# Loads brought forward over layer ends, own credits for up and down, and the last square summed on TensorE, in a two-stack transformer kernel

## What is computed

```python
for l in range(DEPTH):                      # first stack, DEPTH = 2
    h = mixer_sublayer(h, mix_pre_g[l], mix_post_g[l], w_in[l], ..., w_out[l])
    h = ffn_sublayer(h, ffn_pre_g[l], ffn_post_g[l], ffn_w_up[l], ffn_conv_w[l], ffn_w_down[l])
# mixer_sublayer: u = rms_norm(h, pre_g); z = u @ w_in; attention, convolutions; y @ w_out
#                 return h + rms_norm(y, post_g)
# ffn_sublayer:   z = conv(rms_norm(h, pre_g) @ w_up); y = (silu(g) * up) @ w_down
#                 return h + rms_norm(y, post_g)
...
# second stack, per layer: h = h + mixers(_rmsnorm(h, norm_attn_2)) @ w_out_2
#                          h = h + relu(_rmsnorm(h, norm_mlp_2) @ w_up_2) ** 2 @ w_down_2
# output: _rmsnorm(h, final_norm_2)
```

## Time and profile before

| what | value |
|---|---|
| median of 3 runs | 3361.15 us (3355.04 to 3365.78) |
| the profiled execution | 3370.27 us, of it the span 3368.3 us |
| TensorE matmul busy | 88% of the span, 18018 matmuls |
| VectorE, ScalarE, GpSimd busy | 44%, 32%, 8% |
| mean granted clock of TensorE | 0.899 of full speed |
| DMA | 235.90 MB, mean 70 GB/s |
| a 1 MB load of the ring | 4.8 us from issue to landing |

### The profile page before, as it was taken

How to read it: one execution, slowest core, us unless ns; L and a number is a source line. 1 busy time by engine, 2 the same in 40 slices (tenths; PEclk the granted TensorE clock), 3 DMA queues, 4 the chain that set the end, 5 groups by cost and what they waited for, 6 DMA issues and landing times. The chain is left out here.

```text
span 3368.3 us, 47839 instructions
## 1 busy us (share of the span) xinstructions
PE 2973.7 (88%) x18018; PEld 2573.7 (76%) x18018; DVE 1475.2 (44%) x2316; ACT 1066.9 (32%) x1482; POOL 259.1 (8%) x230
## 2 busy tenths in 40 slices
PE   6897899896988899988898886999979878789998
PEld 5886899896986799987695555877768755567776
DVE  3642577613553377722323543423332245433332
ACT  3234433322234333322322223323232222333232
POOL 1000200003000200002000012000010001200001
PEclk8988999998988899999896778999989767789999
DMA  3200322221210322221421001222222200022222
GB/s 111 93 19 26 119 87 87 75 92 52 88 50 1 118 87 89 79 86 38 156 88 38 1 1 50 87 93 95 87 84 97 75 1 1 26 75 87 96 90 76
DMA packets 43930, 235.90 MB, mean 70 GB/s; under 512 B 4286, under 2 KB 14142, under 8 KB 20752
## 3 DMA queue, kind: packets, MB, share of 16 engines
q1 hardware_dynamic: 33968, 220.92, 18.9%
q10 hardware_dynamic: 9824, 13.16, 1.2%
HBM read 231.91 MB, written 11.59 MB: 72 GB/s over the span
## 5 line engine op out<-in xcount | busy, mean ns | idle before, releaser
L163 PE MATMUL psum<-u_up_a_hi,w_a_hi 128*128 128x264 f32 x1408 | 377.8, 288 | 19.9 <-DVE u_up_a_lo L1688 16.9
L164 PE MATMUL psum<-u_up_a_lo,w_a_hi 128*128 128x264 f32 x1408 | 374.0, 286 | 0.0
L154 DVE TENSOR_TENSOR w_mlp_b_lo<-ring,w_mlp_b_hi 128x1024 fp32r<-128x1024 f32 x128 | 156.8, 1225 | 384.5 <-ACT w_mlp_b_hi L147 384.5
L154 DVE TENSOR_TENSOR w_a_lo<-ring,w_a_hi 128x1024 fp32r<-128x1024 f32 x150 | 186.0, 1241 | 254.3 <-ACT w_a_hi L147 251.9
L163 PEld LDWEIGHTS psum<-u_up_a_hi,w_a_hi 128*128 128x128 f32 x1408 | 265.8, 189 | 28.9 <-DVE u_up_a_lo L1688 21.9
L166 PE MATMUL psum<-u_up_a_hi,w_a_lo 128*128 128x264 f32 x1408 | 286.5, 285 | 0.0
L164 PEld LDWEIGHTS psum<-u_up_a_lo,w_a_hi 128*128 128x128 f32 x1408 | 265.2, 188 | 0.2
L147 ACT ACTIVATE w_a_hi<-ring 128x1024 fp32r<-128x1024 f32 x150 | 158.3, 1056 | 320.7 <-PE psum L166 320.5
L147 ACT ACTIVATE w_mlp_b_hi<-ring 128x1024 fp32r<-128x1024 f32 x128 | 136.1, 1063 | 348.5 <-PE psum L166 347.7
L163 PE MATMUL psum<-u_up_b_hi,w_mlp_b_hi 128*128 128x512 f32 x512 | 203.4, 397 | 24.7 <-DVEq L500 24.7
L166 PEld LDWEIGHTS psum<-u_up_a_hi,w_a_lo 128*128 128x128 f32 x1408 | 220.1, 189 | 0.0
(11 more groups left out here) (405 smaller groups left out, 6845.5 us busy)
## 6 DMA issues: line engine op xcount, KB each, us to landing
ring<-in_wup SPq DMA_DIRECT2D x44, 1024.0 KB, 4.8
ring<-in_wup_b SPq DMA_DIRECT2D x32, 1024.0 KB, 4.8
ring<-in_wdown_b SPq DMA_DIRECT2D x32, 1024.0 KB, 4.9
ring<-in_win SPq DMA_DIRECT2D x24, 1024.0 KB, 4.8
ring<-in_wdown SPq DMA_DIRECT2D x32, 704.0 KB, 4.1
ring<-in_win_b SPq DMA_DIRECT2D x16, 1024.0 KB, 4.9
near_copies<-near_rows ACTq DMA_DIRECT2D x2, 4608.0 KB
ring<-in_wout SPq DMA_DIRECT2D x8, 1024.0 KB, 4.8
```

The costliest lines, as they stand in the source:

```text
L154: nc.vector.tensor_tensor(W["lo"][:, buf, 0:n], W["tiles"][:, slot, at:at + n], W["hi"][:, buf, 0:n].bitcast(F32), ALU.subtract).then_inc( ...
L163: nc.tensor.matmul(out[c], a_hi, b_hi, start=start, stop=False)
L164: nc.tensor.matmul(out[c], a_hi, b_lo, start=False, stop=False)
```

## The change

- The ring's two fill semaphores now belong to both stacks and count through. The first stack's down stage and the second stack's last down product load the next layer's first two slots (`win_next`, `win_b_next`); the start stage loads those of the first layer. The constants that used the ring as a staging place get places of their own. The last layer loads two slots that nobody reads.
- The gains of the scaling come from a small table of their own (`pre_gain`), loaded one stage or more ahead. The large column table is waited for after the second low part.
- In the first stage of each layer, the first lot's high part comes before the rounding of h, and its low part after the second scaled tile. The load of ScalarE's table for logarithm and exponential comes after the second high part. The turning of the far rows comes after lot 0.
- Up and down of the second stack have semaphores of their own (`up_free`, `down_free`), down uses banks 4 and 5, and all first credits are given at the beginning of the stage.
- GpSimd sums the first seven squares only; TensorE multiplies the total, then the last square, into the same bank. In `linear_stage` ScalarE squares before it copies.
- In `layer_end_a` VectorE adds to h, one tile behind its scaling.

```diff
-def first_slots(eng, ring, source):
-    for s in range(2):
-        w = source(s)
-        eng.dma_start(ring["tiles"][:, s, 0:w.shape[-1]], w).then_inc(ring["full"][s], 16)
 def slot_full(ring, layer, base, j):
-    return layer * (ring["per_layer"] // 2 * 16) + (j * 16 + (base // 2 + 1) * 16)
+    return layer * (ring["per_layer"] // 2 * 16) + (ring["full_base"] + j * 16 + (base // 2 + 1) * 16)
...
-            pe.wait_ge(added.sem, added.at(layer, 9 * use + 9))
+            pe.wait_ge(added.sem, added.at(layer, KD * use + KD))
             for c, (c0, cn) in enumerate(chunks(T)):
-                mm = nc.tensor.matmul(ps[:, 6 + c, 0:cn], S["mean_mat"][:, :], total[:, c0:c0 + cn], start=True, stop=True)
+                nc.tensor.matmul(ps[:, 6 + c, 0:cn], S["mean_mat"][:, :], total[:, c0:c0 + cn], start=True, stop=False)
+            pe.wait_ge(made.sem, made.at(layer, KD * use + KD))
+            for c, (c0, cn) in enumerate(chunks(T)):
+                mm = nc.tensor.matmul(ps[:, 6 + c, 0:cn], S["mean_mat"][:, :], sq[:, c0:c0 + cn], start=False, stop=True)
             mm.then_inc(summed.sem, 1)
...
-                    nc.scalar.activation(split(out[:, it * tiles + t, 0:T], T), banks(ps, wide * b, T), ACT.Copy)
-                    act.wait_ge(added.sem, added.at(layer, it * tiles + (9 * use + t + 1)))
+                    act.wait_ge(added.sem, added.at(layer, it * tiles + (KD * use + t + 1)))
                     nc.scalar.activation(split(sq[:, 0:T], T), banks(ps, wide * b, T), ACT.Square).then_inc(made.sem, 1)
-                    act.wait_ge(made.sem, made.at(layer, it * tiles + (8 * use + t + 1)))
-                    act.sem_inc(free.sem, 1)
+                    act.wait_ge(made.sem, made.at(layer, it * tiles + (KD * use + t + 1)))
+                    nc.scalar.activation(split(out[:, it * tiles + t, 0:T], T), banks(ps, wide * b, T),
+                                         ACT.Copy).then_inc(free.sem, 1)
...
+    def step(it, last):
+        for t in range(tiles - 1 if last else tiles):
+            pool.wait_ge(made.sem, made.at(layer, it * tiles + (KD * use + t + 1)))
+            pool.wait_ge(added.sem, added.at(layer, it * tiles + (KD * use + t + 1)))
             pass_waits(pool, S)
             nc.gpsimd.tensor_tensor(total, total, sq, ALU.add).then_inc(added.sem, 1)
+    nc.gpsimd.memset(total, 0.0).then_inc(added.sem, 1)
+    in_rounds(pool, rounds, step)
...
-    ps, mm_done, free, w_lo = S["psum"], W["mm_done"], S["psum_free"], W["w_lo"]
+    ps, mm_done, free, w_lo = S["psum"], W["mm_done"], S[L.free], W["w_lo"]
     x_hi, x_lo = L.x
     with pe.Fori(0, L.rounds()) as it:
         for j in range(4):
-            b, first, last = j // L.parts, j % L.parts == 0, (j + 1) % L.parts == 0
+            t, first, last = j // L.parts, j % L.parts == 0, (j + 1) % L.parts == 0
+            b = L.bank + t
             if first:
-                pe.wait_ge(free.sem, free.at(layer, it * L.tiles() + (L.free_base + b + 1)))
+                pe.wait_ge(free.sem, free.at(layer, it * L.tiles() + (L.free_base + t + 1)))
...
+        pe.wait_ge(S["y_added"].sem, S["y_added"].at(layer, KD * L.stats + KD))
+        nc.tensor.matmul(ps[:, 6, :], S["mean_mat"][:, :], S["y_total"][:, :], start=True, stop=False)
+        pe.wait_ge(S["y_sq"].sem, S["y_sq"].at(layer, KD * L.stats + KD))
+        nc.tensor.matmul(ps[:, 6, :], S["mean_mat"][:, :], S["y_square"][:, :], start=False,
                          stop=True).then_inc(S["y_summed"].sem, 1)
...
-            o = h[:, it * L.tiles() + b, :]
-            nc.vector.tensor_tensor(o, ps[:, b, :], o, ALU.add).then_inc(free.sem, 1)
-    if L.ready:
-        dve.wait_ge(free.sem, free.at(layer, L.free_base))
-    dve.sem_inc(free.sem, L.tiles())
+            o = h[:, it * L.tiles() + t, :]
+            nc.vector.tensor_tensor(o, ps[:, L.bank + t, :], o, ALU.add).then_inc(free.sem, 1)
...
-    dve.wait_ge(free.sem, free.at(layer, L.free_base))
-    dve.sem_inc(free.sem, 4)
-    dve.sem_inc(S["sq_out"].sem, 4)
...
+            dve.sem_inc(S[L.free].sem, L.tiles())
             low_of(nc, dve, W, layer, L, 0, 0)
...
+            sp.dma_start(G["pre_gain"][:, :], A["pre_gains"][layer + (DEPTH + 1)]).then_inc(G["gain_in"].sem, 16)
...
+            dve.sem_inc(S["up_free"].sem, 4)
+            dve.sem_inc(S["down_free"].sem, 2)
+            dve.sem_inc(S["sq_out"].sem, 4)
...
+            for slot in range(2):
+                sp.wait_ge(G["full"][slot], DEPTH * (SLOTS_A + SLOTS_B) // 2 * 16 + 16)
         @block.vector
         def _(dve):
-            dve.wait_ge(S["final_in"], 16)
+            dve.wait_ge(gain_in.sem, gain_in.at(DEPTH, DEPTH + 1))
...
-def layer_end_a(nc, S, layer, y, h, gain):
+def layer_end_a(nc, S, G, layer, A, y, h, gain):
+    scaled, added = S["res_scaled"], S["res_added"]
     with nc.Block() as block:
+        @block.sync
+        def _(sp):
+            sp.dma_start(G["pre_gain"][:, :], A["pre_gains"][layer + 1]).then_inc(G["gain_in"].sem, 16)
         @block.vector
         def _(dve):
-            for k in range(KD):
-                add_scaled(nc, dve, S, layer, 1, k, y, gain)
-        @block.gpsimd
-        def _(pool):
-            for k in range(KD):
-                add_to_h(nc, pool, S, layer, 1, k, y, h)
+            for k in range(KD + 1):
+                if k < KD:
+                    add_scaled(nc, dve, S, layer, 1, k, y, gain)
+                if k >= 1:
+                    dve.wait_ge(scaled.sem, scaled.at(layer, KD + k))
+                    nc.vector.tensor_tensor(h[:, k - 1, :], h[:, k - 1, :], y[:, k - 1, :], ALU.add).then_inc(added.sem, 1)
         @block.scalar
         def _(act):
             for k in range(KD):
-                act.wait_ge(S["res_added"].sem, S["res_added"].at(layer, KD + k + 1))
+                act.wait_ge(added.sem, added.at(layer, KD + k + 1))
...
+                sp.dma_start(G["pre_gain"][:, :], A["pre_gains"][0]).then_inc(G["gain_in"].sem, 16)
+                for slot in range(2):
+                    sp.dma_start(ring[:, slot, :], A["win"][0, slot]).then_inc(G["full"][slot], 16)
+                sp.dma_start(staged[:, :], A["fixed_a"]).then_inc(consts_in, 16)
...
-    gain, shaped, shaped_high, shaped_low = col("mix_pre"), S["in_scaled"], S["in_high"], S["in_low"]
+    gain, gain_in = G["pre_gain"], G["gain_in"]
...
-            first_slots(sp, W, lambda j: A["win"][layer, j])
...
+            high(0)
             for k in range(KD):
                 act.wait_ge(shaped.sem, shaped.at(layer, k + 1))
                 nc.scalar.activation(u_hi[:, k, :], scaled_h[:, k, :], ACT.Copy).then_inc(shaped_high.sem, 1)
-                if k == 4:
-                    high(0)
             high(1)
...
-            dve.wait_ge(S["cols_in"].sem, S["cols_in"].at(layer, 1))
+            dve.wait_ge(gain_in.sem, gain_in.at(layer, 1))
...
-                if k == 6:
+                if k == 1:
                     low(0)
             low(1)
+            dve.wait_ge(S["cols_in"].sem, S["cols_in"].at(layer, 1))
...
-                         lambda j: A["wdown"][layer, j], 16, hid, 38, 93, 75, 10 + 48, None, y, 1,
+                         lambda j: A["wdown"][layer, j], 16, hid, 38, 93, 75, 10 + 48, lambda j: A["win_next"][layer, j], y, 1,
                          units=FF_PAIRS // 2, tile_parts=2)
-            layer_end_a(nc, S, layer, y, h, col("ffn_post"))
+            layer_end_a(nc, S, G, layer, A, y, h, col("ffn_post"))
...
-            first_slots(sp, W, lambda j: A["win_b"][layer, j])
...
-            pe.wait_ge(M["turn_in"], 16)
-            pe.wait_ge(S["far_in"].sem, S["far_in"].at(layer, HEADS_B))
-            pass_waits(pe, S)
-            for i in range(4):
-                mm = nc.tensor.matmul(ps[:, 7, P * i:P * (i + 1)], M["far_shifted"][:, P * i:P * (i + 1)],
-                                      M["turn_blocks"][:, :], start=True, stop=True)
-            mm.then_inc(S["far_turned"].sem, 1)
...
+                if p:
+                    continue
+                pe.wait_ge(M["turn_in"], 16)
+                pe.wait_ge(S["far_in"].sem, S["far_in"].at(layer, HEADS_B))
+                pass_waits(pe, S)
+                for i in range(4):
+                    mm = nc.tensor.matmul(ps[:, 7, P * i:P * (i + 1)], M["far_shifted"][:, P * i:P * (i + 1)],
+                                          M["turn_blocks"][:, :], start=True, stop=True)
+                mm.then_inc(S["far_turned"].sem, 1)
...
-            load_ln_and_exp(nc, act)
+            high(0)
             for k in range(KD):
 
                 act.wait_ge(shaped.sem, shaped.at(layer, k + 1))
                 nc.scalar.activation(u_hi[:, k, :], scaled_h[:, k, :], ACT.Copy).then_inc(shaped_high.sem, 1)
-                if k == 4:
-                    high(0)
             high(1)
+            load_ln_and_exp(nc, act)
 
...
-            ups = [Product(lambda j: A["wup_b"][layer, j], 8, u, 20, 62, 32, 12, lambda j: A["wdown_b"][layer, j],
```

(18 more changed lines are left out.)

86 lines of the change are left out of this document (43 added, 43 removed).

## The result

The changed kernel takes 3258.06 us (median of 4 runs, 3247.76 to 3267.45), the kernel before 3358.10 beside it (3353.23 to 3365.78). The ratio is 0.9699, with a 95% interval from 0.9663 to 0.9736: 3.0% faster, 100 us. The prediction was 3262.6, between 3250 and 3286, and faster. The profiled execution took 3267.45 us, its span 3264.5, so the spans differ by 3368.3 - 3264.5 = 103.8 us, against 98.5 in the sum.

What follows compares the result with a forecast made beforehand. TensorE, busy 88% of the span, bounded the kernel, so time could come only from its idle stretches and what they cost behind them. 35.7 + 12.7 + 18.4 + 7.0 + 24.7 = 98.5 us off 3361.15 gave 3262.6, range 3250 to 3286.

Steps and rivals of the forecast that it cites:

- the sum: Whole kernel: the predicted gains added up, 35.7 + 12.7 + 18.4 + 7.0 + 24.7 = 98.5 us.
- Part 1: Second stack's out stage and MLP: early credits and own banks gain 35.7 us at junctions, 12.7 at starts.
- the margin of 0.4 us: Up to down junction: hidden tiles are ready at 2201.83, 0.4 us before the first lot of down ends.
- A short stall costs its length plus 1.7 us: TensorE: a short stall costs its own length plus about 1.7 us, for the low clock in the lot behind.
- Part 2: Out, down and MLP statistics: the last square goes straight to TensorE, gaining 18.4 us, bounds 14 and 21.
- Part 3: First stack's layer end: VectorE both scales and adds, gaining 3.5 us each, 7.0 in all, bounds 5.6 to 8.0.
- Part 4: Layer starts, both stacks: scaling starts earlier and the first lot runs beside it, gaining 24.7 us, bounds 15 and 29.
- Rival A: Layer starts: paced lots stay at the low clock, 2.4 us each, so 3272 us; chance 0.13.
- my own signs of being wrong: Traces: new hidden tile waits, lots at 0.50 over 5 us, additions over 0.76, late VectorE start, late gain or weights.
- Rival C: Second layers' starts: weights' DMAs cause the late first instructions, so 2.9 us gained, not 0.7, twice; 3258; chance 0.06.
- Rival B: Up to down junctions: the second lot of down waits for hidden tiles, four stalls stay, +25.7 us, 3288; chance 0.05.
- Rival D: Attention stages: the granted clock falls and the kernel is slower; a 0.1 fall uses up 98 us; chance 0.02.

Runs made afterwards that it cites:

- written out: The changed kernel with the two loops over the layers written out, so that no engine jumps back: 3241.01 us, ratio 0.9666.
- the delays: The changed kernel with three, or one, extra VectorE subtractions before the hidden tiles' last low part at each up to down junction: 3266.36 us, or 3259.18 us.

## Why the prediction was right, and where it was off

**Part 1** holds in mechanism, and nearly in size. At the junction 5.44 + 5.46 us stand where 4.73 + 7.13 stood; the margin of 0.4 us was measured as 0.36. Undone, the junctions cost 38.1 us (sum: 35.7) and the starts 13.7 (12.7). "A short stall costs its length plus 1.7 us" was the step that is too simple: I had read the price at one junction of each kind and taken it for all. In the kernel before, the four stalls of 4.7 us cost 1.6, 2.7, 1.9 and 2.8 us more than their length, 2.3 on average; that is most of the 2.4 us that the sum lacks. Ones of 0.35 cost 0.3 more, and ones of 1.8 cost 1.9 three times and 0.3 once.

**Part 2**: undone 18.9, sum 18.4. The terms are best read in the two kernels themselves, from the start of TensorE's last weight product to the logarithm. In the first stack that is 6.14 us before and 3.12 after for out, 4.88 and 2.26 for down. In the second stack it is 5.54 and 5.45 (the two layers) and 3.08 for out, 4.63 and 3.08 for the MLP. The gains are 3.0, 2.6, 2.4 and 1.55, 19.2 in all, and only the first of them was mis-sized (2.6). The undone pieces split otherwise because of the clock. In the MLP the product took 2.07 for 1.12 us, so undoing cost 2.7 and not 1.55. In down the local gain is there (from the last eviction to the logarithm 4.56 us before, 1.86 after, where ScalarE squares first), but down's first lot took 14.08 us from its first rounding after and 12.77 before, and gave 1.3 back. The prediction had no term for that; the lot took the shorter time with the change too, three times out of fourteen.

**Part 3**: 3.3 to 3.4 each for 3.5. A step takes 1.30 us (bounds 1.28 and 1.42), and the means end 0.4 us later behind the last square.

**Part 4**: from the logarithm to the end of the first lot (in the second stack the second, so that the turning matmuls are in it both times) the four starts took 25.44, 25.30, 34.23 and 29.49 us before and 17.88, 20.38, 24.73 and 26.52 after. That is 25.0 us for the sum's 24.7. The split was off: the order of the parts is worth 17.9 of it where I had 14.6, so the fetch and the gain by themselves give 7.1 and not 10.1.

Rival A said that lots which are fed slowly stay at the low clock. They did not stay there, but one of my own signs of being wrong did appear, lots at 0.50 for longer than 5 us. In the first stack's second layer TensorE worked without a pause at 0.50 for the first 5.3 us of the lot, from 804.77, and at the full clock from then on. It cost nothing: TensorE had caught up with the input and waited for the low part of the last tile, and the lot ended at 814.65, 15.4 us after VectorE's first instruction. In the second stack TensorE is granted the full clock while it is busy for 2.35 of 3 us. First the slow stretch, then this one (stretch, length, busy time by engine, granted clock):

```profile
806.00:809.00 3.00, 3.00 (x16) 3.00 (x15) 3.00 (x4) 1.25 (x3) 1.72 (x1) 0.50 0.00 0
...
1581.00:1584.00 3.00, 2.35 (x11) 1.31 (x10) 1.96 (x2) 2.94 (x4) 2.19 (x6) 1.00 0.56 199
```

The Trainium skill, TensorE: Matmul & The Clock Gate, section on psum-queue depth-cycling, tells of a bf16 kernel in which frequent small idles between groups of matmuls make the clock swing. In this stretch, with idles of 0.2 to 0.5 us, it did not. Rival C fell in the changed kernel already, where VectorE comes 2.98 us after GpSimd with no load of weights beside it, 2.96 before; written out the lateness is gone. The Trainium skill, Runtime: NRT & Kernel Launch, section Instruction fetch mechanics, says that the target of a taken branch has to be fetched when it is not among the pages at hand. The trace agrees: it shows the fetches behind the jump and none without it, at 3.2 us for a jump over a layer.

**Rival B** fell by the delays. **Rival D** did not happen in its large form, but its mechanism, the granted clock of these stages, is seen in the scatter. I had argued that the attention stages show the same digits in both layers; over more kernels they do not. An attention piece moves by 10 us with nothing changed in it. I counted these stages as unchanged, which was right on average only. So the agreement of the total (3258.1 for 3262.6) is in part luck. The pieces without attention give 59.1 for 59.5, and even there the MLP's 2.6 too much and down's 2.7 too little cancel. Those with attention give 43.4 for 39.0. Of the 43.4 the starts are 25.0, the first stack's out 6.0 and the second's 9.6 (between GpSimd's zeroings 52.04 and 51.17 us before, 47.65 and 45.98 after). The 2.8 that are left stand in the attention. The 1.3 up to the first logarithm are scatter as well: with the same loads ahead that piece took 23.8 to 25.9 us in the runs with the loops. That the total falls on the 3258 of rival C, which did not happen, shows how little a total alone decides here. The bounds of the parts, as they are written, add up to 69 us (with the clock's share of part 1 left out) and 108 us, and not to 73 and 109; the measured gain of 100 lies inside both.

## What to carry to other kernels

Give an engine's credits where nothing is queued ahead of them, at the start of a stage, on resources of their own; then ask which date is the next latest, and measure the margin by a delay. To move the time of one edit out of a scatter that is as large as the edit, cut the span at instructions that every kernel has, and compare pieces rather than totals: two totals here overstated what their edits gave by 10 and some 5 us, and a third agreed with its forecast for the wrong reasons. Whatever fills an engine's gap must end before the work that it waits for is ready, and before a barrier that waits for it.

## What the runs showed of the hardware

- The granted clock of a stage is not a property of its code. The start of the attention ran at 0.60 or 0.85. A stall of 1.8 us was followed by the low clock three times out of four, and at the same place in the code in one layer and not in the other.
- The price of a stall beyond its length, by the lot behind it: 0.3 us for 0.35, 0.3 or 1.9 for 1.8, 1.8 to 1.9 for 3.2, and 1.6 to 3.2 for 4.7.
- A jump back over a layer costs 3.2 us until VectorE's first instruction, 5.02 against 1.82 us after the logarithm, with three fetches of instructions in between, while GpSimd is there 3 us before it.
- An addition of two f32 tiles of 528 columns takes 0.70 us on a VectorE that GpSimd does not disturb, and the next instruction starts 0.62 us after it. Beside GpSimd's addition (1.77) VectorE's scaling takes 1.81 instead of 0.76, so one engine did both in less time than two.
